# GLU groups between the memory attention's steps, and the next head's scores between transposes and values

## The chip, the cores and the metric

One core of one Trainium2 chip runs the whole program. The time is device microseconds (us) of one execution; lower is better. The core has five engines that run their own instruction queues and meet through semaphores: TensorE (PE in the profile), VectorE (DVE), ScalarE (ACT), GpSimd (POOL) and SyncE (SP, which here only issues DMAs). TensorE writes to PSUM (`ps`, eight banks of 512 floats per partition), and VectorE and ScalarE carry results on from there.

## What is computed

One decoder layer for a prompt of 1024 tokens and 32 sample tokens (8 x 4), so 1056 token columns. The part that matters here comes after the input projection: the gated linear unit behind the state-space branch, the cross-attention into 256 memory tokens, and the sparse attention of the prompt.

```python
# state-space branch: y is (tokens, 512), w_glu is (512, 1024)
a, g = jnp.split(y @ w_glu, 2, axis=-1)
o_s = a * jax.nn.sigmoid(g)
# memory attention: 4 heads of 128, 256 keys
s = jnp.einsum('bthd,bmhd->bhtm', q, mk) * (MEM_HEAD_DIM ** -0.5)
o_m = jnp.einsum('bhtm,bmhd->bthd', jax.nn.softmax(s, axis=-1), mv)
# prompt attention: 8 query heads, 2 KV heads of 128; ALiBi; a mask keeps the chosen keys
s = q @ k_sel * (HEAD_DIM ** -0.5) - slopes * dist          # -inf where not valid
o_a = jax.nn.softmax(s, axis=-1) @ v_sel
mix = concat(o_a * silu(gate_a), o_s * silu(gate_s), o_m * silu(gate_m))
```

All of it is float32 in this part of the kernel.

## The kernel before

The program is a row of blocks that each end in a barrier of all engines: setup, project, `mix_a` (`block_c`, from line 1267), `attend` (`block_d`, from line 1502), sample, out. The change touches `mix_a` and `attend`.

**`mix_a`.** SyncE issues all loads at once, in this order: `yT` (the state-space output), the first and the other columns of `w_glu`, the gates `gate_s` (into `mixT`, which lies in `y_room`), `kT`, `vT`, the memory keys and values `mem_kv`, the memory queries `qmT`, `gate_m`, and the attention gates `gate_a`. TensorE then goes through three pieces of work in a fixed order.

1. The GLU (L1370): twelve groups, for four chunks `c` of 128 output columns and the three token pieces of `HALVES` (512, 512 and 32 columns). A group is eight matmuls, four into one bank for `a` and four into the next for `g`. ScalarE takes the sigmoid of `g` (L1427), VectorE multiplies it by `a` (L1457) and into `mixT` (L1465). Two pairs of banks (0 and 1, 2 and 3) are used in turn.
2. The turning of keys and values by token (L1379, copied by ScalarE in L1431) and of the memory keys (L1384, copied by ScalarE in L1433 into `mkT`, a piece of `yT` that the GLU no longer needs).
3. The memory attention, over `s` with one tile of 128 queries each: logits of tile `s` (L1396, four matmuls of 256 columns), values of tile `s - 2` (L1407, eight of 128) and transposes of tile `s - 1` (L1417, eight of 128 x 128). Between them VectorE takes the maximum (L1471) and scales it (L1472), ScalarE takes four exponentials (L1440), VectorE inverts their sums (L1476) and multiplies (L1477), and the transposed weights are copied to `pmT`, one half by ScalarE (L1447) and one by VectorE (L1487). VectorE multiplies the result into `mixT` (L1483). It starts when all of the GLU is done (`glu_used` is waited for in full), since its weights `pm` and `pmT` lie in the room of `w_glu`.

**`attend`.** `UNITS` are 16 pairs of a query tile `t` (0 to 7) and a KV head `g`; unit `u` has `t + 1` key blocks. Step `s` computes the scores of unit `s`, one head `j` after the other (L1666, 128 queries against `(t + 1) * 128` keys); VectorE adds the distances, finds the maximum and writes `lg` (L1730), ScalarE writes the exponentials `pr` (L1697). Beside it unit `s - 1` is finished, cut into four parts by `steps`: "turn" a key block (L1641, four transposes into bank 4 or 5), have it copied to `prT` (L1683, blocks with even number by ScalarE, odd ones by VectorE), and "value" it (L1651, one matmul of 512 columns). A block's values follow one transpose later in TensorE's order. When a unit's values are done VectorE multiplies them into `mixT` (L1740), and GpSimd scales them by the inverse sums (L1631), which SyncE moves through DRAM. On that queue of SyncE also stand the loads of the queries two tiles on (`load_queries`, L1499) and the first loads of the sample block.

What orders ScalarE's queue in `attend`:

```python
for s in range(len(UNITS) + 1):
    for j in range(GQA):
        ...  # exponential of head j of unit s, waits for VectorE's s_read
        copy_turned(act, nc.scalar.copy, s - 1, todo[j], 0)
```

Of the kernel before, what the change touches and what calls it, by code (L numbers as in the profile page):

```python
# [16 lines left out]
P = 128  # L17
# [16 lines left out]
HALVES = [(0, 512), (512, 512), (SEQ, NS)]  # L34
# [12 lines left out]
SPAN = 8  # L47
# [1219 lines left out]
def block_c(nc, io, v, sem, sb_in):  # L1267
# [4 lines left out]
    with own:  # L1272
# [6 lines left out]
        sg = sb("sg", [P, 2, 512])  # L1279
        ag = sb("ag", [P, 512])  # L1280
# [20 lines left out]
        GLU = [(c, n) for c in range(4) for n in range(3)]  # L1301

# [57 lines left out]
        def _(pe):  # L1360
            pe.wait_ge(glu_loaded, 48)
            for i, (c, n) in enumerate(GLU):
                t0, w = HALVES[n]
                if (c, n) == (1, 0):
                    pe.wait_ge(glu_rest, 32)
                if i >= 2:
                    pe.wait_ge(glu_used, i - 1)
                for a in range(2):
                    for k in range(4):
                        last = nc.tensor.matmul(ps[:, 2 * (i % 2) + a, 0:w], w_glu[:, k, a * D_SSM + c * P:a * D_SSM + (c + 1) * P],  # L1370
                                                yT[:, k, t0:t0 + w], start=(k == 0), stop=(k == 3))
                last.then_inc(glu_mm, 1)
            pe.wait_ge(kv_loaded, 32)
# [14 lines left out]
            pe.wait_ge(glu_used, len(GLU))  # L1388
            pe.wait_ge(kv_copied, QT + 1)
            for s in range(QT + 2):  # L1390
                if s < QT:

                    if s >= 2:
                        pe.wait_ge(exp_done, 4 * (s - 1))
                    for h in range(N_MEM_HEADS):
                        last = nc.tensor.matmul(ps[:, 2 * (s % 2) + h // 2, (h % 2) * N_MEM:(h % 2 + 1) * N_MEM],  # L1396
                                                qmT[:, h, s * P:(s + 1) * P], mkT[:, h, :], start=True, stop=True)
                    last.then_inc(s_mm, 1)
                if s >= 2:
                    u = s - 2  # L1400
                    for k in range(2):
                        pe.wait_ge(p_copied[k], u + 1)
                    if u >= 2:
                        pe.wait_ge(o_used, u - 1)
                    for h in range(N_MEM_HEADS):
                        for k in range(2):
                            last = nc.tensor.matmul(ps[:, 6 + u % 2, h * P:(h + 1) * P], mem_kv[:, 1, k, h * P:(h + 1) * P],  # L1407
                                                    pmT[:, u % 2, k, h, :], start=(k == 0), stop=(k == 1))
                    last.then_inc(o_mm, 1)
                if 1 <= s <= QT:  # L1410
                    u = s - 1
                    pe.wait_ge(p_ready, u + 1)
                    for k in range(2):
                        if u >= 1:
                            pe.wait_ge(p_copied[k], u)
                        for h in range(N_MEM_HEADS):
                            last = nc.tensor.transpose(ps[:, 4 + k, h * P:(h + 1) * P], pm[:, u % 2, h, k * P:(k + 1) * P], ident[:])  # L1417
                        last.then_inc(p_turned, 1)

        @block.scalar  # L1420
        def _(act):
            for i, (c, n) in enumerate(GLU):
                w = HALVES[n][1]
# [3 lines left out]
                nc.scalar.activation(sg[:, i % 2, 0:w], ps[:, 2 * (i % 2) + 1, 0:w], ACT.Sigmoid).then_inc(glu_sig, 1)  # L1427
            for t in range(QT + 1):
                n = P if t < QT else NS
                act.wait_ge(kv_turned, t + 1)  # L1430
                nc.scalar.activation(kv_tok[0:n, t, :], ps[0:n, 4 + t % 2, :], ACT.Copy).then_inc(kv_copied, 1)  # L1431
            act.wait_ge(mk_turned, 1)
            nc.scalar.activation(yT[:, 0, 0:4 * N_MEM], ps[:, 6:8, :].rearrange("p a n -> p (a n)"), ACT.Copy).then_inc(mk_copied, 1)  # L1433
            for s in range(QT + 1):
                if s < QT:
# [3 lines left out]
                    for h in range(N_MEM_HEADS):  # L1439
                        nc.scalar.activation(pm[:, s % 2, h, :], ps[:, 2 * (s % 2) + h // 2, (h % 2) * N_MEM:(h % 2 + 1) * N_MEM],  # L1440
                                             ACT.Exp, bias=nb[:, s, h:h + 1], scale=SCALE, accum_out=rs[:, s, h:h + 1]).then_inc(exp_done, 1)
                if s >= 1:
                    u = s - 1
                    act.wait_ge(p_turned, 2 * u + 1)
                    if u >= 2:
                        act.wait_ge(o_mm, u - 1)
                    nc.scalar.activation(pmT[:, u % 2, 0, :, :].rearrange("p h n -> p (h n)"), ps[:, 4, :], ACT.Copy).then_inc(p_copied[0], 1)  # L1447

        @block.vector
        def _(dve):  # L1450
            link = v["dve_chain"].on(dve)
            TSC, TT = nc.vector.tensor_scalar, nc.vector.tensor_tensor
            dve.wait_ge(gate_s_loaded, 32)
            for i, (c, n) in enumerate(GLU):
                t0, w = HALVES[n]
                dve.wait_ge(glu_sig, i + 1)
                TT(ag[:, 0:w], ps[:, 2 * (i % 2), 0:w], sg[:, i % 2, 0:w], ALU.mult).then_inc(glu_used, 1)  # L1457
                dve.wait_ge(glu_used, i + 1)
                if n < 2:
                    o = mixT[:, 8 + c, 0:SEQ].rearrange("p (k j) -> p j k", j=SPAN)[:, t0 // BLKS:(t0 + w) // BLKS, :]  # L1460
                    x = ag[:, 0:w].rearrange("p (j k) -> p j k", k=BLKS)
                else:
                    o = mixT[:, 8 + c, SEQ:TOK].rearrange("p (b q) -> p q b", q=DEC_SEQ)
                    x = ag[:, 0:w].rearrange("p (q b) -> p q b", q=DEC_SEQ)
                link(TT(o, o, x, ALU.mult))  # L1465
            dve.wait_ge(gate_m_loaded, 32)
            for s in range(QT + 2):
                if s < QT:
                    dve.wait_ge(s_mm, s + 1)
                    src = ps[:, 2 * (s % 2):2 * (s % 2) + 2, :].rearrange("p a (h n) -> p (a h) n", h=2)  # L1470
                    link(nc.vector.tensor_reduce(nmx[:, s, :], src, AX_X, ALU.max, negate=True))  # L1471
                    TSC(nb[:, s, :], nmx[:, s, :], SCALE, None, ALU.mult).then_inc(nb_ready, 1)  # L1472
                if 1 <= s <= QT:
                    u = s - 1
                    dve.wait_ge(exp_done, 4 * (u + 1))
                    link(nc.vector.reciprocal(rinv[:, u, :], rs[:, u, :]))  # L1476
                    TT(pm[:, u % 2, :, :], pm[:, u % 2, :, :], rinv[:, u, :].unsqueeze(2).to_broadcast([P, 4, N_MEM]),  # L1477
                       ALU.mult).then_inc(p_ready, 1)
                if s >= 2:
                    u = s - 2  # L1480
# [3 lines left out]
                if 1 <= s <= QT:  # L1484
                    u = s - 1
                    dve.wait_ge(p_turned, 2 * u + 2)
# [1097 lines left out]
```

## Time and profile before

| | us |
|---|---|
| median of 3 runs (1938.87 to 1942.88) | 1939.59 |
| the profiled execution | 1938.08 |
| its span in the profile | 1936.3 |
| of it: GLU, 1154.07 to 1219.08 | 65.0 |
| turning of keys and memory keys, to 1227.03 | 8.0 |
| memory attention, to 1279.5 | 52.5 |
| prompt attention, 1280.5 to 1469.7 | 189.2 |

TensorE is busy for 93% of the span, VectorE for 52%, ScalarE for 42%, GpSimd for 15%. Engines are read as follows: a row of the time line gives the start, the duration, the engine, the line and the operation, and in brackets the idle time before it with what ended it. A matmul of float32 appears as two records. The records of TensorE overlap: the time between two starts is what one costs in a stream, and the duration of the last one holds its drain. PEclk is the share of TensorE's full clock of 2.4 GHz that was granted.

### The profile page before, as it was taken

The page shows a single profiled execution, that of the slowest core. Times are in us where ns is not written, and L with a number is a line of the kernel's source. Part 1 is how long each engine was busy: PE and PEld are TensorE (multiplying, and loading weights), DVE is VectorE, ACT ScalarE, POOL GpSimd, SP SyncE. Part 2 cuts the span into 40 slices and gives each one's busy share as a digit, 9 for nine tenths or more (in the row PEclk, how much of TensorE's full clock was granted, in tenths as well). Part 3 has the DMA queues.
Part 4 walks back from the last instruction along what each step waited for, and adds up shares of the span by engine and source line. Part 5 has one row for each costly group of instructions (what it writes and reads, how often), then busy time and mean ns, then how long its engine had stood idle before and what let it go on. Part 6 is the DMA issues. An engine that isn't in the chain of part 4 may idle for free. (4 is left out here: it accounts for less than half of the span.)

```text
span 1936.3 us, 30854 instructions
## 1 busy us (share of the span) xinstructions
PE 1802.8 (93%) x12571; PEld 1217.1 (63%) x12571; DVE 1013.2 (52%) x1945; ACT 817.3 (42%) x1386; POOL 294.0 (15%) x202
## 2 busy tenths in 40 slices
PE   6969999999999999999999979779889679999997
PEld 4555555556666666666666645664545368888886
DVE  5544126547978677687785602454435542222326
ACT  5454457764444334343433300444334744333431
POOL 3012220111121111111221100144103000000000
PEclk9989999999999999999999989989999799999999
DMA  9422221212223222222222146213215622222224
GB/s 331 141 88 66 72 66 34 67 45 78 74 70 94 80 75 78 80 84 78 78 74 75 51 149 253 67 26 85 66 34 158 205 67 67 89 67 67 68 89 180
DMA packets 193679, 179.82 MB, mean 93 GB/s; under 512 B 30658, under 2 KB 173154, under 8 KB 190786
## 3 DMA queue, kind: packets, MB, share of 16 engines
q1 hardware_dynamic: 174338, 140.29, 23.8%
q10 hardware_dynamic: 14640, 22.96, 3.2%
q0 software_dynamic: 4560, 14.58, 2.3%
q8 instruction: 101, 1.65, 0.4%
q14 instruction: 40, 0.33, 0.1%
HBM read 143.59 MB, written 34.20 MB: 92 GB/s over the span
## 5 line engine op out<-in xcount | busy, mean ns | idle before, releaser
L670 PE MATMUL ps<-h,w 128*128 128x352 f16 (+2 forms) x6096 | 943.9, 315 | 6.5 <-POOL w L950 6.1
L670 PEld LDWEIGHTS ps<-h,w 128*128 128x128 f16 (+1 forms) x6096 | 595.5, 99 | 337.9 <-issue 15.4
L950 POOL TENSOR_TENSOR w<-wb,w 128x2048 f16<-128x2048 f32 (+1 forms) x45 | 186.6, 4147 | 840.6 <-ACT w L802 840.6
L2372 PE MATMUL ps<-w_f,m 128*128 128x256 f16 x2688 | 297.0, 273 | 3.1 <-DVE y_room L2439 3.1
L2372 PEld LDWEIGHTS ps<-w_f,m 128*128 128x128 f16 x2688 | 263.1, 98 | 35.6 <-issue 4.6
L1152 DVE MAX8 m<-score 128x8 f32<-128x1024 f32 (+2 forms) x192 | 171.6, 894 | 5.7
L1153 DVE MATCH_REPLACE8 score<-m,score 128x1024 f32<-128x1024 f32 (+2 forms) x192 | 168.1, 876 | 0.0
L810 ACT ACTIVATE zst<-ps,unit 128x352 f32<-128x352 f32 (+1 forms) x88 | 50.0, 583 | 250.8 <-PE ps L670 226.7
L2454 DVE SCALAR_TENSOR_TENSOR y_room<-ps,unit_f,x_f 128x256 f32<-128x256 f32 (+1 forms) x64 | 30.6, 483 | 225.5 <-PE ps L2372 195.8
L1144 DVE SCALAR_TENSOR_TENSOR score<-room,wis,score 128x1024 f32<-128x1024 f32 (+5 forms) x90 | 92.7, 1030 | 78.6 <-ACT room L872 73.3
L798 ACT ACTIVATE wb<-wb,unit 128x2048 f32<-128x2048 f32 (+1 forms) x45 | 89.5, 1989 | 91.6 <-DVE unit L967 91.6
L784 ACT ACTIVATE absolute<-wb 128x512 bf16<-128x512 f32 (+1 forms) x180 | 112.5, 625 | 9.7 <-PEq L209 6.0
L872 ACT ACTIVATE room<-ps,qk_unit 128x1024 f32<-128x1024 f32 (+5 forms) x96 | 76.5, 845 | 54.9 <-PE ps L691 54.3
L1697 ACT ACTIVATE pr<-lg,nmx_d 128x128 f32<-128x128 f32 (+7 forms) x64 | 49.6, 776 | 107.7 <-DVE nmx_d L1730 107.3
L2515 ACT ACTIVATE qi_s<-y_room 128x256 bf16<-128x256 f32 (+3 forms) x72 | 29.6, 412 | 146.2 <-DVE y_room L2454 143.3
L1651 PE MATMUL ps<-prT,kv_tok 128*128 128x512 f32 x144 | 75.5, 612 | 15.5 <-ACT prT L1683 12.8
L802 ACT ACTIVATE w<-wb 128x2048 f16<-128x2048 f32 (+1 forms) x45 | 85.4, 1898 | 4.0
L1666 PE MATMUL ps<-kT,v_or_q 128*128 128x512 f32 (+3 forms) x192 | 75.4, 508 | 7.1 <-DMA v_or_q<-z_scratch 4.6
L1730 DVE CUSTOM_DVE_ANT_0 lg<-dist,ps 128x384 f32<-128x384 f32 (+5 forms) x48 | 42.6, 887 | 70.7 <-PE ps L1666 70.4
L1370 PE MATMUL ps<-yT,w_glu_sb 128*128 128x512 f32 (+1 forms) x192 | 65.2, 503 | 13.5 <-DMA w_glu_sb<-in_w_glu_dram 13.5
L961 DVE TENSOR_REDUCE unit<-ps 128x1 f32<-128x4 f32 x45 | 7.2, 161 | 117.6 <-PE ps L653 117.2
L1370 PEld LDWEIGHTS ps<-yT,w_glu_sb 128*128 128x128 f32 x192 | 32.7, 196 | 46.3 <-issue 32.4
(456 smaller groups left out, 1848.3 us busy)
## 6 DMA issues: line engine op xcount, KB each, us to landing
wb<-in_w_in_dram SPq DMA_DIRECT2D x44, 1024.0 KB, 5.2
z_scratch<-zst ACTq DMA_DIRECT2D x32, 528.0 KB, 2.7
score<-in_w_out_dram SPq DMA_DIRECT2D x7, 2048.0 KB, 11.5
y_room<-z_scratch SPq DMA_DIRECT2D x8, 1056.0 KB, 18.0
x_in<-in_x_prompt_dram SPq DMA_DIRECT2D x8, 1024.0 KB, 7.3
w_kv<-in_w_mem_kv_dram POOLq DMA_DIRECT2D x16, 512.0 KB, 5.3
x_f<-in_x_prompt_dram SPq DMA_DIRECT2D x8, 1024.0 KB, 5.3
out_y_p_dram<-y_room SPq DMA_DIRECT2D x8, 1024.0 KB, 3.9
```

What stands on the lines that cost most here:

```text
L670: last = nc.tensor.matmul(ps[0:m, n, 0:w], w16[:, b, pw_, k, 0:m], h16[:, ph, k, t0:t0 + w], start=(k == 0 and i == 0), stop=(k == KT - 1 ...
L784: nc.scalar.activation(absolute[:, :, 0:w], wb[:, b, 4 * k:4 * k + 4, 0:w], ACT.Abs, accum_out=size[:, b, k:k + 1]).then_inc(w_summed, 1)
L798: nc.scalar.activation(src, src, ACT.Copy, scale=unit[:, c % 4, 1:2]).then_inc(act_link, 1)
L802: nc.scalar.activation(high, src, ACT.Copy).then_inc(w_high, 1)
L872: nc.scalar.activation(rel[:, a, 0:(t + 1) * P], src, ACT.Relu, scale=qk_unit[:, 1 + i:2 + i]).then_inc(act_read, 1)
L950: nc.gpsimd.tensor_tensor(w16[:, b, 1, :, 0:w], wb[:, b, :, 0:w], w16[:, b, 0, :, 0:w], ALU.subtract).then_inc(w_split, 1)
L1144: STT(out=sc, in0=r, scalar=wi, in1=sc, op0=ALU.mult, op1=ALU.add).then_inc(acc_done, 1)
L1152: link(nc.vector.max(out=m8[:], in_=sc))
L1153: link(nc.vector.match_replace(out=sc, in_to_replace=m8[:], in_values=sc, imm_value=REPLACED))
L1370: last = nc.tensor.matmul(ps[:, 2 * (i % 2) + a, 0:w], w_glu[:, k, a * D_SSM + c * P:a * D_SSM + (c + 1) * P], yT[:, k, t0:t0 + w], start= ...
L1651: nc.tensor.matmul(ps[:, 6 + u % 2, :], v_, prT[:, gk % 2, :, :].rearrange("p j n -> p (j n)"), start=(k == 0), stop=(k == t)).then_inc(o_ ...
L2372: last = nc.tensor.matmul(ps[:, bank(b, t), 0:SLAB], m16[:, mp, k, t * P:(t + 1) * P], weights(s, b, wp, k), start=(k == 0 and j == 0), st ...
```

## The change

In `mix_a` the token pieces of the GLU become 384, 384 and 288 columns. Three of its twelve groups stay ahead of the memory attention (two before the turning of keys and values, one after), and one of the other nine stands in each of the nine steps of the memory attention, between the transposes of tile `s - 1` and its values, which now belong to the same step. All groups but the second use banks 2 and 3, and the logits have banks 0 and 1 alone. `mkT`, `pm` and `pmT` move out of `yT` and `w_glu`: `mkT` to the unused end of `y_room`, `pm` to `k_room`, `pmT` (now one buffer in place of two) to the room of the memory keys. Sigmoids and exponentials alternate on ScalarE. In `attend` a block's values come after the next head's scores, VectorE's product with the gate moves to the start of the next step but one, and there is one step more.

```diff
-HALVES = [(0, 512), (512, 512), (SEQ, NS)]
+THIRDS = [(0, 384), (384, 384), (768, 256 + NS)]
...
-        mkT = yT[:, 0, 0:4 * N_MEM].rearrange("p (h n) -> p h n", h=4)
-
-        pm = w_glu[:, 0:2, :].rearrange("p b (h n) -> p b h n", h=4)
-        pmT = w_glu[:, 2:4, :].rearrange("p b (k h n) -> p b k h n", k=2, h=4)
+        mkT_flat = v["y_room"][:, KT * TOK:KT * TOK + 4 * N_MEM]
+        mkT = mkT_flat.rearrange("p (h n) -> p h n", h=4)
+
+        pm = v["k_room"][:].rearrange("p (b h n) -> p b h n", b=2, h=4)
+        pmT = mem_kv[:, 0, :, :].rearrange("p k (h n) -> p k h n", h=4)
...
+        GLU_FIRST = 3
+        def glu_bank(i):
+            return 0 if i == 1 else 2
...  # TensorE: glu(i) as before, but
-                    pe.wait_ge(glu_used, i - 1)
+                    pe.wait_ge(glu_used, i)
...
+            pe.wait_ge(glu_loaded, 48)
+            glu(0)
+            glu(1)
             pe.wait_ge(kv_loaded, 32)
...
+            glu(2)
             pe.wait_ge(mem_loaded, 64)
...
-            pe.wait_ge(glu_used, len(GLU))
             pe.wait_ge(kv_copied, QT + 1)
-            for s in range(QT + 2):
+            for s in range(QT + 1):
                 if s < QT:
-                    ...  # logits(s), values(s - 2), transposes(s - 1)
+                    logits(s)
+                if s:
+                    turn(s - 1)
+                glu(GLU_FIRST + s)
+                if s:
+                    values(s - 1)
...  # ScalarE, in a step: copy of tile s - 1 to pmT, four exponentials of tile s, then
+                gate(GLU_FIRST + s)
...  # VectorE, in a step: maximum of tile s, copy to pmT, inverse sums and product of tile s, then
+                multiply(GLU_FIRST + s)
+                if s >= 1:
+                    ...  # product of tile s - 1 into mixT
...  # attend
-        def steps(u):
-            ...
+        STEPS = len(UNITS) + 2
+        def blocks(u, j):
+            if not 0 <= u < len(UNITS):
+                return []
             kb = UNITS[u][0] + 1
+            return [(u, k) for k in range(kb * j // GQA, kb * (j + 1) // GQA)]
+        def turned_at(s, j):
+            return blocks(s - 1, j)
+        def valued_at(s, j):
+            return turned_at(s, j - 1) if j else turned_at(s - 1, GQA - 1)
...  # TensorE, after the scores of head j
-                    if s and j == 0:
+                    for u, k in valued_at(s, j):
+                        value(u, k)
+                    if j == 0 and 1 <= s <= len(UNITS):
                         pe.wait_ge(exp_done, GQA * s)
-                    for kind, k in todo[j]:
-                        (turn if kind == "turn" else value)(s - 1, k)
+                    for u, k in turned_at(s, j):
+                        turn(u, k)
...  # VectorE, after the copies of part j
+                    if j == 0 and s >= 2:
+                        gate(s - 2)
-                if s:
-                    ...  # the same product, for unit s - 1, at the end of step s
```

## Rows read from the trace of the kernel before

**Rows 1.** Busy time by stage: us, PE, PEld, DVE, ACT, POOL, PEclk, DMA share, GB/s.
```profile
1154.07:1219.08 65.01, 65.01 (x193) 32.60 (x193) 14.49 (x22) 5.38 (x11) 0.00 (x0) 0.96 0.60 235
1219.08:1227.03 7.95, 5.98 (x46) 4.57 (x46) 1.46 (x3) 6.18 (x12) 1.80 (x1) 1.00 0.02 4
1227.03:1279.50 52.47, 40.69 (x256) 36.56 (x256) 31.70 (x47) 21.39 (x73) 3.76 (x2) 0.93 0.20 61
1280.50:1331.44 50.94, 44.19 (x161) 25.58 (x162) 26.05 (x89) 24.25 (x72) 34.52 (x57) 0.93 0.30 70
1331.44:1469.70 138.26, 123.46 (x465) 67.26 (x463) 58.09 (x110) 48.87 (x93) 24.46 (x13) 0.99 0.23 51
```

**Rows 2.** Waits of PE, 1154 to 1280: who for whom, us, times, longest.
```profile
PE ps L1417 <- DVE w_glu_sb L1477: 10.1, 7, 3.6
```

**Rows 3.** Time line of PE in one step of the memory attention.
```profile
1241.75 1.10 PE L1417 MATMUL ps<-ident,w_glu_sb 128*128 128x128 f32 x8 [1.08 <-DVE w_glu_sb L1477]
1242.68 1.89 PE L1396 MATMUL ps<-yT,qmT 128*128 128x256 f32 x8
1244.41 1.95 PE L1407 MATMUL ps<-w_glu_sb,mem_kv 128*128 128x128 f32 x16
```

**Rows 4.** Time line of ACT: the sigmoids of the first three GLU groups.
```profile
1164.12 0.60 ACT L1427 ACTIVATE sg<-ps 128x512 f32<-128x512 f32 x1 [18.52 <-PE ps L1370]
1170.99 0.60 ACT L1427 ACTIVATE sg<-ps 128x512 f32<-128x512 f32 x1 [6.27 <-PE ps L1370]
1172.69 0.20 ACT L1427 ACTIVATE sg<-ps 128x32 f32<-128x32 f32 x1 [1.11 <-PE ps L1370]
```

**Rows 5.** Busy time by stretch, as rows 1: PEclk after two waits of PE.
```profile
1154.00:1158.00 4.00, 3.93 (x5) 1.85 (x6) 0.00 (x0) 0.00 (x0) 0.00 (x0) 0.50 1.08 382
1234.40:1238.50 4.10, 4.10 (x15) 3.54 (x16) 0.69 (x1) 0.88 (x3) 0.00 (x0) 0.58 0.94 307
```

**Rows 6.** Time line of SP's queue: when two of the loads are issued.
```profile
1153.14 0.46 SPq L1322 DMA_DIRECT2D v_or_q<-z_scratch  x1
1157.60 5.06 SPq L1327 DMA_DIRECT2D qmT<-z_scratch  x2
```

**Rows 7.** DMA issues of the same loads: KB each, us from issue to landing.
```profile
v_or_q<-z_scratch SPq DMA_DIRECT2D x1, 1056.0 KB, 16.1
qmT<-z_scratch SPq DMA_DIRECT2D x2, 1056.0 KB, 16.9
```

**Rows 8.** Time line of ACT: the table load ahead of the first exponential.
```profile
1227.00 1.28 ACT L1440 ACT_TABLE_LOAD   x1
1230.92 0.47 ACT L1440 ACTIVATE w_glu_sb<-ps,nb_c 128x256 f32<-128x256 f32 x1 [2.65 <-DVE nb_c L1472]
```

**Rows 9.** Groups by line, memory attention: count, busy us, mean ns, idle before.
```profile
L1471 DVE TENSOR_REDUCE nmx_c<-ps 128x4 f32<-128x1024 f32 x8 | 9.8, 1225 | 16.1 <-PE ps L1396 16.1
L1440 ACT ACTIVATE w_glu_sb<-ps,nb_c 128x256 f32<-128x256 f32 x32 | 14.7, 476 | 22.5 <-DVE nb_c L1472 22.5
```

**Rows 10.** Waits of PE in the prompt attention, 1331 to 1470.
```profile
PE ps L1651 <- ACT prT L1683: 12.2, 10, 2.2
```

**Rows 11.** Time line of PE, DVE and ACT at one of these waits.
```profile
1440.59 1.04 PE L1641 MATMUL ps<-ident,pr 128*128 128x128 f32 x8
...
1440.79 1.22 DVE L1730 CUSTOM_DVE_ANT_0 lg<-dist,ps 128x1024 f32<-128x1024 f32 x1 [1.03 <-PE ps L1666]
...
1442.06 1.15 ACT L1697 ACTIVATE pr<-lg,nmx_d 128x1024 f32<-128x1024 f32 x1 [3.68 <-DVE nmx_d L1730]
...
1443.82 0.70 PE L1651 MATMUL ps<-prT,kv_tok 128*128 128x512 f32 x1 [2.19 <-ACT prT L1683]
```

**Rows 12.** Groups by line and shape, prompt attention: the 640-key head.
```profile
L1730 DVE CUSTOM_DVE_ANT_0 lg<-dist,ps 128x640 f32<-128x640 f32 x8 | 6.6, 822 | 8.6 <-PE ps L1666 8.5
L1697 ACT ACTIVATE pr<-lg,nmx_d 128x640 f32<-128x640 f32 x8 | 6.6, 830 | 11.6 <-DVE nmx_d L1730 11.5
```

**Rows 13.** Time line of PE: the first scores of tile 3.
```profile
1314.73 1.12 PE L1666 MATMUL ps<-kT,v_or_q 128*128 128x512 f32 x2 [1.24 <-DMA v_or_q<-z_scratch]
```

More of the change, by code:

```diff
@@ L1360, in _, with glu @@
         def _(pe):
-            pe.wait_ge(glu_loaded, 48)
-            for i, (c, n) in enumerate(GLU):
-                t0, w = HALVES[n]
+            def glu(i):
+                c, n = GLU[i]
+                t0, w = THIRDS[n]
                 if (c, n) == (1, 0):
@@ L1387, in _, with gate @@
             pe.wait_ge(mk_copied, 1)
-            pe.wait_ge(glu_used, len(GLU))
             pe.wait_ge(kv_copied, QT + 1)
-            for s in range(QT + 2):
+            for s in range(QT + 1):
                 if s < QT:
[L1393 to L1418, printed above, removed]
+                    logits(s)
+                if s:
+                    turn(s - 1)
+                glu(GLU_FIRST + s)
+                if s:
+                    values(s - 1)
         @block.scalar
         def _(act):
-            for i, (c, n) in enumerate(GLU):
-                w = HALVES[n][1]
+            def gate(i):
+                w = THIRDS[GLU[i][1]][1]
                 act.wait_ge(glu_mm, i + 1)
@@ L1452, in _, with multiply @@
             TSC, TT = nc.vector.tensor_scalar, nc.vector.tensor_tensor
-            dve.wait_ge(gate_s_loaded, 32)
[L1454 to L1465, printed above, removed]
+            def multiply(i):
+                c, n = GLU[i]
+                t0, w = THIRDS[n]
+                dve.wait_ge(glu_sig, i + 1)
+                TT(ag[:, 0:w], ps[:, glu_bank(i), 0:w], sg[:, i % 2, 0:w], ALU.mult).then_inc(glu_used, 1)
+                dve.wait_ge(glu_used, i + 1)
+                w_p = min(w, SEQ - t0)
+                o = mixT[:, 8 + c, 0:SEQ].rearrange("p (k j) -> p j k", j=SPAN)[:, t0 // BLKS:(t0 + w_p) // BLKS, :]
+                x = ag[:, 0:w_p].rearrange("p (j k) -> p j k", k=BLKS)
+                last = TT(o, o, x, ALU.mult)
+                if w_p < w:
+                    o = mixT[:, 8 + c, SEQ:TOK].rearrange("p (b q) -> p q b", q=DEC_SEQ)
+                    x = ag[:, w_p:w].rearrange("p (q b) -> p q b", q=DEC_SEQ)
+                    last = TT(o, o, x, ALU.mult)
+                link(last)
@@ L1466, in _ @@
+            dve.wait_ge(gate_s_loaded, 32)
+            for i in range(GLU_FIRST):
+                multiply(i)
             dve.wait_ge(gate_m_loaded, 32)
-            for s in range(QT + 2):
+            for s in range(QT + 1):
                 if s < QT:
                     dve.wait_ge(s_mm, s + 1)
-                    src = ps[:, 2 * (s % 2):2 * (s % 2) + 2, :].rearrange("p a (h n) -> p (a h) n", h=2)
+                    src = ps[:, 0:2, :].rearrange("p a (h n) -> p (a h) n", h=2)
                     link(nc.vector.tensor_reduce(nmx[:, s, :], src, AX_X, ALU.max, negate=True))
@@ L1652, in value @@
                                  start=(k == 0), stop=(k == t)).then_inc(o_mm, 1)
-            for s in range(len(UNITS) + 1):
-                todo = steps(s - 1) if s else [[]] * 4
+            for s in range(STEPS):
                 for j in range(GQA):
@@ L1668, in _, with copy_turned @@
                         last.then_inc(s_mm, 1)
-                    if s and j == 0:
+                    for u, k in valued_at(s, j):
+                        value(u, k)
+                    if j == 0 and 1 <= s <= len(UNITS):
                         pe.wait_ge(exp_done, GQA * s)
-                    for kind, k in todo[j]:
-                        (turn if kind == "turn" else value)(s - 1, k)
-        def copy_turned(eng, copy, u, todo, parity):
-            for kind, k in todo:
+                    for u, k in turned_at(s, j):
+                        turn(u, k)
+        def copy_turned(eng, copy, todo, parity):
+            for u, k in todo:
                 gk = first_key_block[u] + k
-                if kind == "turn" and gk % 2 == parity:
+                if gk % 2 == parity:
                     eng.wait_ge(p_turned, gk + 1)
@@ L1687, in _ @@
             for s in range(len(UNITS) + 1):
-                todo = steps(s - 1) if s else [[]] * 4
                 for j in range(GQA):
@@ L1713, in invert, with gate @@
                 nc.vector.reciprocal(rinv[:, GQA * u:GQA * (u + 1)], rs[:, GQA * u:GQA * (u + 1)]).then_inc(rinv_ready, 1)
-            for s in range(len(UNITS) + 1):
-                todo = steps(s - 1) if s else [[]] * 4
+            def gate(u):
+                t, g = UNITS[u]
+                dve.wait_ge(o_mm, first_key_block[u + 1])
+                o = mixT[:, GQA * g:GQA * (g + 1), t * P:(t + 1) * P]
+                nc.vector.tensor_tensor(o, o, ps[:, 6 + u % 2, :].rearrange("p (j n) -> p j n", j=GQA), ALU.mult).then_inc(o_used, 1)
+            for s in range(STEPS):
                 for j in range(GQA):
```

90 lines of the change are left out of this document (52 added, 38 removed).

## The prediction

> **What bounds the kernel now.** I read the stages by busy time first [rows 1]. Both stages that the change touches are TensorE's, and in both it stops for short times. In the GLU it never stops: 65.01 us busy in 65.01. In the memory attention it is busy for 40.69 of 52.47 us, and the clock is 0.93. In the prompt attention after 1331.44 it is busy for 123.46 of 138.26. Then the waits, to see on whom: in the memory attention on VectorE's product with the inverse sums (10.1 us) [rows 2], in the prompt attention mostly on ScalarE's copy of transposed weights (12.2 us) [rows 10]. So the softmax of a tile, or the copy of a block, has too little of TensorE's work beside it. The GLU is such work, 65 us with no stop, and stands ahead of the attention that could use it.
>
> **The GLU's own cost.** A 512-column group takes 1170.99 - 1164.12 = 6.87 us from sigmoid to sigmoid, a 32-column group 1172.69 - 1170.99 = 1.70 [rows 4]. Eight and four of them are 61.8 us; the 3.2 us that are left of 65.01 are the start at half clock (0.50) after the wait for the first loads [rows 1, 5], and stay. The new pieces by columns: 384 cost 5.15, 288 cost 3.87; eight and four are 56.7. Gain **5.1**.
>
> **The memory attention's steps.** From start to start the transposes take 0.93 us and the logits 1.73 [rows 3]; the values have as many columns as the logits, so 1.73 too (their 1.95 holds the drain that follows them now). A step's own work is 4.39 us, eight tiles 35.1, against 52.47 us now [rows 1]: **17.4** go if the GLU group in each step covers all waits. Does it? A step is 4.39 + 5.15 = 9.54 us, or 8.26 with a 288-column group. The softmax chain of a tile: logits 1.73, maximum 1.23, four exponentials of 0.476, product 1.23 (an estimate: as many elements as the maximum) [rows 9], some five hand-overs of 0.20 each as between TensorE and VectorE [rows 11]: 7.1 us. Its result is wanted by the next step's transposes, at 8.26 + 1.73 = 10.0 at the earliest. Covered by 2.9 us.
>
> What is added in a step: on ScalarE a sigmoid and two table switches, since sigmoid and exponential each load a table now; one load takes 1.28 us. The load at 1227.00 ran ahead of the wait of its exponential, which began at 1230.92 [rows 8], so I expect the loads in ScalarE's idle time; even with one on the chain it is 8.4 against 10.0. ScalarE's sum is 1.9 + 0.45 + 2.56 + 0.6 for the copy (an estimate from what follows the exponential in rows 11) = 5.5 of 8.26 us. That row speaks for hidden switches. The Trainium skill, "ScalarE: Activation LUTs", section "Table sets: the hidden batching unit", speaks against them: calls are to be batched by set, and a switch is budgeted at about 2.7 us, by which ScalarE's sum would be 8.3, just over the short step. The trace has 1.28 for the load itself; the rule as a result of its own is the second rival.
>
> The new waits: TensorE waits for VectorE's product of the last GLU group (`glu_used`), since all later groups share banks 2 and 3. Behind it are the values and the next logits. The group ends 7.81 us into a step; sigmoid and product follow by about 9.5 (they stand behind the softmax product of 7.1 to 8.4), and the next group begins at 8.26 + 2.66 = 10.9 or later. Covered by 1.4 us or more. Behind VectorE's wait for the sigmoid stand the gate product of tile s - 1 and the next maximum; the latter has until 9.99. Covered, thinly.
>
> The loads: two GLU groups in front take 3.2 + 10.3 us from 1154.07, to 1167.6. `vT` lands at 1153.14 + 16.1 = 1169.2 [rows 6, 7]: a new wait of about **1.7** us that the long GLU hid. `qmT` lands by about 1177.3 (its second half is issued 2.5 us into the row) [rows 6, 7]; the turning (7.95) [rows 1] and the third group put the first logits at 1167.6 + 1.7 + 7.95 + 3.87 = 1181.1 and the turning of the memory keys, which waits for it, some 2 us earlier. Hidden by 1.8 us. After a wait of 3.6 us the clock fell to 0.58 [rows 2, 5], so the 1.7 us may cost up to 2 more. Values at 1.95 instead of 1.73 would take 1.8. The same tail as now remains at the end. Sum 5.1 + 17.4 - 1.7 = 20.8; with part of these bounds I take **20** (16 to 21).
>
> SyncE's and GpSimd's queues only have the attention gates, the queries and the scaling of `kT`, which start earlier and end before the stage does. The moved rooms cost no instruction.
>
> **The prompt attention.** From the end of the scores to the values that wait for ScalarE's copy it takes 1443.82 - 1440.59 = 3.23 us at 1024 keys (VectorE 1.22, exponential 1.15, copy and hand-overs the rest); eight transposes cover 1.04 of it, and the wait is 2.19 [rows 11]. After the change the previous blocks' values, this part's transposes and the next head's scores lie between. By 1.73 us for 1024 columns [rows 3] a block's values (512 columns) are 0.865, scores 0.216 for 128 keys, and a block's transposes about 0.44 [rows 11]. At 1024 keys two blocks a part: 1.73 + 0.88 + 1.73 = 4.34 against 3.23. Covered. At 640 keys one block: 0.865 + 0.44 + 1.08 = 2.39, against 3.23 less the difference of both engines (0.40 + 0.32) [rows 11, 12] = 2.51: short by 0.1. So about nothing remains but small waits at tiles 4 and 5, some 1 us in all. In the last step no scores are left: a part's values wait for a copy behind one transposed block, about 0.5 us for each of four parts, 2 us.
>
> The sum from 1331.44: scores 8 heads x (5 + 6 + 7 + 8) x 0.216 = 44.9; 56 blocks' transposes x 0.44 = 24.6; values 57 x 0.865 = 49.3 (one more, since they lag); waits 3: 121.8, against 138.26: **16.5**. From the other side: busy 123.46 [rows 1] plus 3 and 0.9 is 127.4, a gain of 10.9; but busy time holds the drain before each wait, which goes with it. I take **15.5**, near the first.
>
> Before 1331.44 I expect nothing. The scores of tile 3 wait for their queries [rows 13], and what TensorE saves before it waits there: SyncE's queue reaches these loads behind GpSimd's set-up work, which does not change. After it the cover at 512 keys (0.865 + 0.44 + 0.86 = 2.17) is about what the chain needs (2.27 by the same differences), so waits like today's stay. Bounds -2 to +1.5 us; value 0. VectorE's gate product moves in front of the second head of a step; there it delays that head's maximum by up to 0.3 us in the middle tiles. The block ends with the same product and GpSimd's scaling. The later stages start earlier and are unchanged.
>
> **Sum.** 20 + 15.5 = 35.5. The profiled execution took 1938.08 (span 1936.3), 1.5 below the median 1939.59; so 1902.6 for that one and **1904** for the median.
>
> **Rivals.**
> - Forecast, 1904, own range 1898 to 1910: chance 0.62.
> - The prompt attention keeps half its waits: VectorE's order (maximum, copies, gate product) or the scores' own semaphore makes ScalarE's copy late again. For it: the margin at 640 keys is below zero and 0.35 at 896; against: 1.1 us at 1024, where most waits are. Half of 15.5: 1912. Chance 0.17.
> - The table switches lie on the path: 16 more loads x 1.28 = 20.5 us [rows 8]: 1924.5. Against it, the load that ran ahead of its wait. Chance 0.07. The Trainium skill's rule (above) names this outcome; by its 2.7 us it would be 43 us, and no gain at all.
> - The loads fall behind and each us late is a us of waiting, or the clock falls in the turning: up to 6 us, 1910. Chance 0.10.
> - Slower than before: the one pair of banks. If each of nine groups had to wait for VectorE's product of the last, TensorE would stop in every step, and after 3.6 us it ran near half clock for 4 us (0.58, some 1.7 us lost) [rows 5]. Nine waits of 3 us with that loss are 42 us: 1946. It decides from 35.5 / 9 = 3.9 us per step, loss included, and needs VectorE 1.4 us of margin plus 2.2 late. Chance 0.04.
>
> That the change doesn't do what it says is hardly possible; the order of the instructions is written out.
>
> The range for 8 in 10 reaches from the forecast's low end over the second and fourth rival: 1898 to 1914. This kernel's measurement tells about 0.2% (4 us) from no change; faster 0.95, same 0.01, slower 0.04.
>
> **What would show it.** The stretch from the first GLU matmul to the last values should take about 105.5 us (125.4 now), with TensorE busy for all but some 3 us and no wait on VectorE's product; some 17 table loads on ScalarE, none ahead of a wait of TensorE; one wait for `vT` of about 1.7 us. In the prompt attention the waits on ScalarE's copy should fall from 12.2 us to about 3, most of them in the last step, and tile 3 should begin 34 us into the block as now. I am wrong if TensorE waits for `glu_used` or for a sigmoid in the steps, if the waits on the copy move to VectorE's, or if the clock in the steps is below 1.00.

## The result, and the profile after

| | before | after |
|---|---|---|
| median us (runs) | 1939.23 (1938.10 to 1942.88, 4) | 1904.77 (1902.38 to 1906.13, 4) |
| profiled execution, span | 1938.08, 1936.3 | 1904.64, 1903.0 |
| first GLU matmul to last values of the memory attention | 125.4 | 106.1 |
| from there to the first matmul of the stage after the prompt attention | 193.2 | 177.2 |
| all that follows | 463.6 | 465.4 |

After / before is 0.9823, with a 95% interval of 0.9810 to 0.9836: 34.5 us gained. By the stages of the two traces it is 19.3 and 16.0, less 1.8 lost in stages that the change doesn't touch. Of the 19.3 some 3 us are the clock in the trace of before, as shown below under "Luck".

Busy time by stage in the kernel after (start:end, us, then busy us and count of PE, PEld, DVE, ACT, POOL, then PEclk, DMA share, GB/s): first two GLU groups and the turning of keys and values; third group and steps; the prompt attention up to the first scores of tile 4; the rest of it. Rows 1 has the stages of before.

```profile
1154.29:1176.35 22.06, 18.44 (x68) 11.80 (x69) 2.82 (x4) 5.48 (x10) 0.00 (x0) 0.86 1.04 402
1176.35:1260.36 84.01, 82.89 (x426) 64.35 (x424) 45.35 (x71) 47.12 (x101) 5.55 (x2) 1.00 0.32 116
1261.49:1312.47 50.98, 44.55 (x158) 24.21 (x159) 25.78 (x88) 25.40 (x72) 34.29 (x57) 0.93 0.32 69
1312.47:1434.88 122.41, 120.92 (x468) 67.66 (x466) 59.54 (x111) 49.08 (x94) 24.66 (x13) 1.00 0.25 58
```

The second line is the merged stage: TensorE is busy for 82.89 of 84.01 us at full clock, where the memory attention alone had 40.69 of 52.47 at 0.93 [rows 1]. The last is 122.41 us, against 138.26 [rows 1].

The waits of TensorE in the kernel after (engine, line, releaser: us in total, times, longest), first for 1154 to 1262, then for 1262 to 1450:

```profile
PE ps L1421 <- DMA v_or_q<-z_scratch: 3.3, 1, 3.3
PE ps L1386 <- ACT y_room L1459: 1.1, 1, 1.1
...
PE ps L1691 <- ACT prT L1724: 3.9, 8, 0.9
PE ps L1705 <- DMA v_or_q<-z_scratch: 1.7, 2, 1.1
PE ps L1691 <- DVE prT L1724: 0.7, 3, 0.3
```

The 10.1 us for VectorE's product [rows 2] are gone, and no line for `glu_used` or a sigmoid has come. The 12.2 us for ScalarE's copy, which rows 10 count from tile 4 on, are 1.4 there (after 1312.47). The other 2.5 of the 3.9 us lie ahead of tile 4, where before had 0.6; there the wait for queries fell in turn, from 4.6 to 1.7. What is new is 3.3 us for `vT`.

One step of the memory attention on TensorE, DVE and ACT (start, us, engine, line, operation, with idle time before it and its releaser in brackets):

```profile
1207.19 1.89 PE L1386 MATMUL ps<-y_room,qmT 128*128 128x256 f32 x8
1208.92 1.04 PE L1397 MATMUL ps<-ident,k_room 128*128 128x128 f32 x8
1209.80 5.33 PE L1377 MATMUL ps<-yT,w_glu_sb 128*128 128x384 f32 x16
1214.96 1.95 PE L1408 MATMUL ps<-mem_kv 128*128 128x128 f32 x16
1216.74 1.89 PE L1386 MATMUL ps<-y_room,qmT 128*128 128x256 f32 x8
...
1209.12 1.23 DVE L1505 TENSOR_REDUCE nmx_c<-ps 128x4 f32<-128x1024 f32 x1 [0.28 <-PE ps L1386]
1210.38 0.17 DVE L1506 TENSOR_SCALAR nb_c<-nmx_c 128x4 f32<-128x4 f32 x1
1213.64 1.22 DVE L1516 TENSOR_TENSOR k_room<-k_room,rinv_c 128x1024 f32<-128x1024 f32 x1
...
1209.56 0.60 ACT L1466 ACTIVATE mem_kv<-ps 128x512 f32<-128x512 f32 x1 [2.71 <-PE ps L1397]
1210.17 1.28 ACT L1472 ACT_TABLE_LOAD   x1
1211.47 0.47 ACT L1472 ACTIVATE k_room<-ps,nb_c 128x256 f32<-128x256 f32 x1
1213.42 1.28 ACT L1449 ACT_TABLE_LOAD   x1
1215.16 0.49 ACT L1449 ACTIVATE sg<-ps 128x384 f32<-128x384 f32 x1 [0.46 <-PE ps L1377]
```

TensorE's five lines follow each other with no bracket: 1216.74 - 1207.19 = 9.55 us for the step. The chain goes beside them: the product (L1516) ends at 1214.86, and the next transposes want it at 1216.74 + 1.73 = 18.47. The exponential's load starts behind ScalarE's copy (L1466) and ends 0.9 us after the scaled maximum (1210.55), so this load is partly on the chain; 3.6 us of margin absorb it. The thinnest place is VectorE's: it waits only 0.28 us for these logits, as forecast ("thinly").

One 1024-key head of the prompt attention after the change, the same columns; rows 11 has it before:

```profile
1404.57 1.22 DVE L1775 CUSTOM_DVE_ANT_0 lg<-dist,ps 128x1024 f32<-128x1024 f32 x1 [1.03 <-PE ps L1705]
1405.83 1.15 ACT L1737 ACTIVATE pr<-lg,nmx_d 128x1024 f32<-128x1024 f32 x1 [2.59 <-DVE nmx_d L1775]
1406.08 1.04 PE L1681 MATMUL ps<-ident,pr 128*128 128x128 f32 x8
1406.95 1.88 PE L1705 MATMUL ps<-kT,v_or_q 128*128 128x512 f32 x4
1406.98 0.56 ACT L1724 COPY prT<-ps 128x512 f32<-128x512 f32 x1
1408.67 1.88 PE L1691 MATMUL ps<-prT,kv_tok 128*128 128x512 f32 x4
```

The copy (L1724) still stands behind the exponential on ScalarE and ends at 1407.54. But the values that need it start at 1408.67, behind the next head's scores, and don't wait.

### The profile page after: what moved, and what is told of

It is laid out like the page before. It is cut to its first block and busy times, and to the rows that moved or that the text cites. A ratio compares the mean times of both kernels' runs of the same rounds, so it can differ in the third digit from the quotient of the medians.

```text
span 1903.0 us, 30882 instructions
## 1 busy us (share of the span) xinstructions
PE 1793.9 (94%) x12571; PEld 1221.9 (64%) x12571; DVE 1014.7 (53%) x1949; ACT 837.6 (44%) x1402; POOL 293.8 (15%) x202
## 5 line engine op out<-in xcount | busy, mean ns | idle before, releaser
L1377 PE MATMUL ps<-yT,w_glu_sb 128*128 128x384 f32 (+1 forms) x192 | 60.1, 468 | 13.4 <-DMA w_glu_sb<-in_w_glu_dram 13.4
L990 DVE SCALAR_TENSOR_TENSOR room<-ps,room 128x400 f16<-128x400 f32 (+1 forms) x16 | 8.9, 558 | 93.8 <-ACT room L818 53.2
```

## The experiments

All medians are of timed runs beside the kernel before; the ratio is against it, with its 95% interval. The rows come from three sets of runs, and the result from a fourth; the median of before was 1939.1 (mix_alone to no_switch), 1938.5 (two_more_switches, copies_first, kv_sooner, three_more), 1938.4 (the other three) and 1939.2 us (the result). Differences between sets are uncertain by that much beside their spread.

| kernel | us | ratio |
|---|---|---|
| mix_alone | 1922.13 | 0.9917 (0.9900 to 0.9934) |
| attend_alone | 1921.19 | 0.9905 (0.9889 to 0.9922) |
| glu_ahead | 1921.29 | 0.9912 (0.9895 to 0.9928) |
| no_switch | 1903.48 | 0.9810 (0.9794 to 0.9827) |
| two_more_switches | 1913.86 | 0.9873 (0.9855 to 0.9891) |
| copies_first | 1926.68 | 0.9935 (0.9916 to 0.9954) |
| mix_and_copies | 1904.47 | 0.9832 (0.9816 to 0.9848) |
| after_copies_first | 1904.02 | 0.9823 (0.9807 to 0.9840) |
| kv_sooner | 1902.25 | 0.9810 (0.9794 to 0.9826) |
| queries_sooner | 1901.64 | 0.9812 (0.9796 to 0.9829) |
| three_more | 1897.31 | 0.9783 (0.9767 to 0.9800) |

**Are the two parts independent?** mix_alone has the diff's part up to the memory attention, attend_alone its part in the prompt attention.

> The kernel before with only the change of the first block: GLU groups in the memory attention's steps, the prompt attention as before. Theory: the two stages gain apart from each other; the stretch from the first GLU matmul to the last values falls from 125.4 to 106.1 us and nothing later changes, so 1939.2 - 19.3 = 1920 (1918 to 1922). Rival: the stages depend on one another (the prompt attention starts on queries that are loaded at a fixed time, so part of the gain is waited for there): 1925 or more.

> The kernel before with only the change of the prompt attention. Theory: the wait for ScalarE's copies goes, 12.2 us to about 4, and the block takes 173.4 in place of 189.3 us: 1939.2 - 16 = 1923 (1921 to 1925), with nothing gained before the scores of tile 4. Rival: part of the 16 us came from the first block's change (its earlier end moves transfers away): 1928 or more.

They gained 17.0 and 17.9 us. The first, 1922.13, is just outside the range expected for it. Together they make 34.9, against 34.5 for the whole change: within the spread of some 3 us, neither part needs or spoils the other.

**Is it the GLU beside the attention, or the new order of a step?** glu_ahead keeps the step's new order, its rooms and its pieces, but puts all twelve groups in front:

```diff
-            return 0 if i == 1 else 2
+            return 2 * (i % 2)
...
-            glu(0)
-            glu(1)
+            for i in range(len(GLU)):
+                glu(i)
...
-                glu(GLU_FIRST + s)
```

> The changed kernel, but all twelve GLU groups ahead of the turning of keys and values, with two pairs of banks in turn; the steps have the new order (logits, transposes of the tile before, its values) and no GLU in them. Theory: the groups' cover is the gain; without it a step is bound by the softmax chain (logits 1.73, maximum 1.23, table-free exponentials 1.9, hand-overs, then the next logits wait for the exponentials): about 5.5 us a step as before (5.7), so the 14 us of the steps are lost again and the thinner pieces' 5 us stay: 1918 to 1922. Rival: the new order of the steps and the shorter lag did it, and the place of the groups matters little: 1905 to 1908.

It gained 17.8, as attend_alone does: with the GLU in front, nothing of the 17 us of mix_alone shows in the medians. In the trace the GLU takes 59.05 us instead of 65.01 and the memory attention 53.86 (before 52.47 [rows 1]). From the first GLU matmul to the last values it is 120.7 us, 4.7 less than in the trace of before, but only 1.4 less than in that of attend_alone (122.1), which has the code of before there. One step of it, TensorE and the VectorE instructions that matter:

```profile
1250.12 1.04 PE L1397 MATMUL ps<-ident,k_room 128*128 128x128 f32 x8
1252.45 2.02 PE L1408 MATMUL ps<-mem_kv 128*128 128x128 f32 x16 [1.29 <-issue]
1254.31 1.89 PE L1386 MATMUL ps<-y_room,qmT 128*128 128x256 f32 x8
...
1250.32 1.23 DVE L1502 TENSOR_REDUCE nmx_c<-ps 128x4 f32<-128x1024 f32 x1 [0.45 <-PE ps L1386]
1251.66 0.69 DVE L1509 COPY mem_kv<-ps 128x512 f32<-128x512 f32 x1
```

The values (L1408) wait 1.29 us. The profile names no releaser here, but VectorE's copy of the second half of the transposed weights (L1509) ends at 1252.35, 0.1 us ahead of them, and it stood behind the maximum; for the waits of 1.33 and 1.34 us of two earlier tiles it names this copy. The new order alone shows no gain; its waits are hidden only where a group lies in them.

**Do the table loads cost anything?** no_switch:

```diff
-                ... ACT.Sigmoid).then_inc(glu_sig, 1)
+                ... ACT.Exp).then_inc(glu_sig, 1)
```

> The changed kernel with an exponential in place of the sigmoid in the GLU's gate, which leaves the sigmoid out and with it all 16 added table loads (20.5 us of ScalarE). Theory: ScalarE has 3 to 4 us to spare in each step and the loads are hidden: 1904.8, within 1. Rival: the loads lengthen the chain to TensorE by 0.8 us or more a step: 1898 or less.

1903.48 against 1904.77: no difference that these runs can tell (their spread is 4 us). The traces are closer: from the first logits to the last values no_switch takes 77.98 us and after 77.97. 16 loads of 1.28 us, 20.5 us in all, are hidden. How near to the edge? two_more_switches puts two loads more on every tile's chain:

```diff
                         nc.scalar.activation(pm[:, s % 2, h, :], ... ACT.Exp, ...).then_inc(exp_done, 1)
+                        if h == 1:
+                            nc.scalar.activation(spare_col[:], ident[:, 0:1], ACT.Sigmoid)
```

> The changed kernel with one more sigmoid of one column between the second and the third exponential of each of the eight tiles; its result is not used. It adds two table loads and about 0.3 us, 2.9 us a step, in the middle of the softmax chain, where they can't run ahead. Theory: VectorE's round of a step (maximum, scaling, the exponentials waited for, inverse, product, GLU product twice, gate product) takes about 8 us of 9.5 or 8.3, so 0.3 us are free in a short step and 1.5 in a long one; 2.9 more cost some 1.5 us in each long and 2.6 in each short step, 12 to 15 us: 1917 to 1920. Rival 1: the cover is wide (the product is wanted only 2.3 us later than it is there), at most 3 us: 1905 to 1908. Rival 2: ScalarE's loads are on TensorE's path already, so all of it is paid: 8 x 2.9 = 23 us, 1928.

It lost 9.1 us against after, where 12 to 15 were expected and the nearest rival had at most 3. TensorE's waits are before the logits, since one pair of banks holds them and the last exponential must have read it:

```profile
PE ps L1387 <- ACT k_room L1473: 5.2, 4, 1.7
PE ps L1398 <- DVE k_room L1519: 1.9, 1, 1.9
```

A loop through VectorE and ScalarE now sets the step. DVE and ACT of one step, with the maximum of the step before it, show it:

```profile
1206.38 1.22 DVE L1508 TENSOR_REDUCE nmx_c<-ps 128x4 f32<-128x1024 f32 x1
1216.33 1.22 DVE L1508 TENSOR_REDUCE nmx_c<-ps 128x4 f32<-128x1024 f32 x1
1222.66 0.18 DVE L1518 RECIPROCAL rinv_c<-rs_c 128x4 f32<-128x4 f32 x1 [4.32 <-ACT k_room L1473]
1224.46 0.56 DVE L1488 TENSOR_TENSOR ag<-ps,sg 128x384 f32<-128x384 f32 x1 [0.37 <-ACT sg L1450]
1226.57 1.22 DVE L1508 TENSOR_REDUCE nmx_c<-ps 128x4 f32<-128x1024 f32 x1
...
1215.82 1.28 ACT L1473 ACT_TABLE_LOAD   x1
1217.78 0.47 ACT L1473 ACTIVATE k_room<-ps,nb_c 128x256 f32<-128x256 f32 x1 [0.68 <-DVE nb_c L1509]
1218.82 1.28 ACT L1476 ACT_TABLE_LOAD   x1
1220.11 0.20 ACT L1476 ACTIVATE spare_col<-ident 128x1 f32<-128x1 f32 x1
1220.32 1.28 ACT L1473 ACT_TABLE_LOAD   x1
```

From maximum to maximum it is 10.24 us in this step, which has a 384-column group, and 9.95 in the one before it, which has 288 columns; VectorE waits for ScalarE alone. Less the 2.9 us of the added chain (two loads and the small sigmoid) that is about 7.3 and 7.1, so the 9.55 us step had 2.2 free and the 8.27 us step 1.2. The loss is 0.7 us in a long and 1.7 in a short step, where 1.5 and 2.6 were expected. My expectation counted only VectorE's idle time ahead of the maximum (0.28 above). It missed that a later maximum takes the exponential's own load off the chain: the load now ends at 1217.10, before the wait (0.68 idle), where it cost 0.9 us in after. 0.28 + 0.9 is the 1.2 of the short step.

**What made the copies late in the prompt attention?** The prediction laid the wait to the length of the chain, to be covered by TensorE's work. The rival: the copy is ready to go long before, and stands behind an exponential on ScalarE that waits for VectorE. copies_first changes the kernel before in that one point and leaves TensorE's order as it was:

```diff
+                    copy_turned(act, nc.scalar.copy, s - 1, todo[j], 0)
                     if s < len(UNITS):
                         n = (UNITS[s][0] + 1) * P
...
-                    copy_turned(act, nc.scalar.copy, s - 1, todo[j], 0)
```

> The kernel before with one edit in the prompt attention: ScalarE's copies of a part stand ahead of the exponential of its head, not behind it. Theory: the waits of TensorE came from the place of the copy behind an exponential; with it gone a value waits 0.8 us less the 0.44 of one transposed block, so the 12.2 us fall to about 5 and the block gains about 7: 1930 to 1933. Rival: what lacks is work of TensorE between transposes and values, whatever ScalarE's order; the exponential, now later, holds up the next tile instead: 1938 to 1941.

It gained 11.8 us; I expected about 7. TensorE's waits from 1331 to 1456, and one head's time line:

```profile
PE ps L1651 <- DVE prT L1683: 2.6, 5, 1.1
PE ps L1651 <- ACT prT L1683: 1.2, 5, 0.2
...
1428.14 1.04 PE L1641 MATMUL ps<-ident,pr 128*128 128x128 f32 x8
1428.77 0.58 ACT L1683 COPY prT<-ps 128x512 f32<-128x512 f32 x1 [2.85 <-PE ps L1641]
1429.41 1.13 PE L1651 MATMUL ps<-prT,kv_tok 128*128 128x512 f32 x2 [0.24 <-ACT prT L1683]
```

The copy runs 0.63 us after the first transposes begin, in time in which ScalarE was idle anyway (2.85), and the values wait 0.24 us instead of 2.19 [rows 11]. Of 12.2 us [rows 10] 1.2 are left. I had expected part of the wait to stay for the chain, and hardly any did. mix_and_copies puts this beside the other half of the change, with TensorE's order in the prompt attention left as before:

```diff
 (mix_alone, and in the prompt attention of before:)
+                    copy_turned(act, nc.scalar.copy, s - 1, todo[j], 0)
                     if s < len(UNITS):
```

> The kernel before with the first block's change and, in the prompt attention, only ScalarE's copies put ahead of the exponentials; TensorE's order there is that of before. Theory: the copy's place behind the exponential made nearly all of the waits, and either cure removes them; the block takes 177.6 us from its first score to the next block's first matmul against 176.1 with the new order of TensorE: 1904.8 + 1.5 = 1906 (1904 to 1909). Rival: TensorE's order gives more once the first block ends 19 us sooner, since other transfers then fall into the block: 1912 or more.

1904.47 against 1904.77 for the change: the same total. The prompt attention itself isn't the same. From its first scores to the next stage's first matmul the traces have:

| kernel | us |
|---|---|
| before | 192.1 |
| mix_alone (order of before) | 191.2 |
| copies_first | 177.6 |
| mix_and_copies | 179.2 |
| attend_alone (new order) | 176.0 |
| after (new order) | 176.1 |

The moved line gives 14.5 us of the 16.2 that the new order gives, and beside the first block's change 12.0 of 15.1. The medians of the two alone differ as well (1926.68 and 1921.19). In the two traces the totals come out level because the later stages of mix_and_copies took 461.3 us, against 465.4 in after. What the new order covers besides is the waits for VectorE's copies: 2.6 us from tile 4 on, in before as in copies_first (above) and in mix_and_copies, and none there in after:

```profile
PE ps L1687 <- DVE prT L1719: 2.6, 5, 1.1
```

after_copies_first has both cures (the copy's line moved as above, in the kernel after):

> The changed kernel with ScalarE's copies ahead of the exponentials. Theory: of the 3.9 us of waits for copies that are left, 2.5 us lie at tiles 1 and 2, where the queries bound the start of the next tile, so little of them is won: 1903 to 1905, and the waits for queries grow from 1.7 to 3 us or more. Rival: all of them go: 1901 or less.

1904.02: no more than the new order alone. Its waits on the copy fell from 3.9 to 1.4 us, and the one for the queries rose from 1.7 to 4.8:

```profile
PE ps L1705 <- DMA v_or_q<-z_scratch: 4.8, 2, 2.6
PE ps L1691 <- ACT prT L1724: 1.4, 6, 0.2
```

Nearly all of those 2.5 us (2.3) were at tiles 1 and 2, where the loads set the pace, so they came back at once.

**The waits for loads.** kv_sooner issues `kT` and `vT` ahead of the state-space gates; queries_sooner issues each tile's queries one unit earlier:

```diff
+            sp.dma_start(kT[:], pair(OFF_K)).then_inc(kv_loaded, 16)
+            sp.dma_start(vT[:], pair(OFF_V)).then_inc(kv_loaded, 16)
             for s in range(2):
                 sp.dma_start(mixT[:, 8 + 2 * s:10 + 2 * s, :], pair(OFF_GS + SLAB * s)).then_inc(gate_s_loaded, 16)
...
-                if g == 0 and 1 <= t < QT - 1:
-                    sp.wait_ge(s_mm, N_HEADS * t)
-                    load_queries(sp, q_t, z_dram, t + 1, q_loaded)
+                if g == 1 and t + 2 < QT:
+                    sp.wait_ge(s_mm, N_HEADS * (t + 1))
+                    load_queries(sp, q_t, z_dram, t + 2, q_loaded)
```

> The changed kernel with the loads of keys and values issued ahead of the GLU's gates. Theory: the wait of 3.3 us for the values and the half clock after it go (about 1 us more); the third group then ends before the memory queries are there, about 1.5 us of waiting comes back: 2.5 to 3 us less, 1902. Rival: the GLU's product, whose gates now land 5 us later, holds up the third group: no change, 1904.8 or more.

> The changed kernel with the queries of the tile after next issued one unit sooner on SyncE's queue. Theory: the 1.7 us of waits for queries go and nothing else: 1903 (1902 to 1904.5). Together with the run before, less than the 5 us that both edits gave on top of the sooner keys: each needs the other, since the copies and the queries bound the first tiles in turn. Rival: the two edits add up, and this one gives 2.5 us or more: 1902 or less.

Against after they gained 2.5 and 3.1 us; by the ratios it is 2.5 and 2.1. The first is within the spread of the runs (1900.1 to 1905.2, against 1902.4 to 1906.1); the runs of the second (1901.2 to 1901.9) all lie below those of after. Its median is below the range expected for it and in that of its rival, but the trace shows the 1.7 us of the theory and no more. The traces agree that both gain. With kv_sooner the 3.3 us for `vT` are gone and a wait of 1.1 us for `qmT` is new:

```profile
PE ps L1427 <- DMA qmT<-z_scratch: 1.1, 1, 1.1
```

With queries_sooner no wait for queries is left, and the prompt attention takes 174.4 us instead of 176.1, first scores to the next stage's first matmul. three_more has both, and the copies first:

> The changed kernel with three edits of order: keys and values loaded ahead of the GLU's gates, the queries of the tile after next issued one unit sooner on SyncE's queue, and ScalarE's copies ahead of the exponentials. Theory: besides the 3 us of the loads, the 4.6 us of waits for copies and the 1.7 us for queries at the first tiles shrink by about 4 together: 1897 to 1900. Rival: at the first tiles the chain from scores to exponential bounds, and a later exponential costs what the sooner copy gives: 1902, as with the loads alone.

1897.31 (1894.1 to 1899.0): 7.5 us less than the change, and the best of all. The single gains (2.5, 3.1 and 0.8) make 6.4. The prompt attention takes 170.8 us, 3.6 less than with queries_sooner alone, though kv_sooner (176.3) and after_copies_first (176.3) left it as it was: with the queries there in time, the copies' place pays, which it could not in after_copies_first. So the edits don't simply add up, and the rival of queries_sooner falls.

## Why the prediction was right, point by point

| term | predicted | measured in the trace of after |
|---|---|---|
| first two GLU groups | 13.5 | 11.99 |
| wait for `vT` | 1.7 | 3.33 |
| turning, third group, memory keys | 11.8 | 12.78 |
| steps | 35.1 + 42.5 = 77.6 | 77.97 |
| first GLU matmul to last values | 105.5 (104.6 by the terms above) | 106.1 |
| tile 3 into its block | 34 | 33.9 |
| prompt attention from tile 4 | 121.8 | 122.41 |
| later stages | unchanged | 1.8 longer |
| profiled execution | 1902.6 | 1904.64 |

- **Steps.** The step at 1.73 us for 1024 columns, with the drain left out, was right to 0.4 us in 78; the bound of 1.8 for slower values was not used. TensorE is busy for all of 77.97 us.
- **The wait for `vT`** is the mis-sized term: 3.33 for 1.7. The load landed as computed from rows 6 and 7 (1169.6 against 1169.2). The two groups in front took 1.5 us less, since the start at half clock cost less than the 3.2 us taken from before: the granted clock of the first 4 us is 0.61 instead of 0.50 [rows 5]. In the four us behind those it is 1.00 instead of 0.76. With the landing fixed the two errors cancel. What doesn't cancel is the clock after the wait, for which the prediction had up to 2 us: 0.75 and then 0.56 in the next 5 us, and the stretch to the first logits 1.0 us longer than forecast. Stretches of the kernel after, columns as above:

```profile
1169.60:1172.00 2.40, 2.14 (x13) 1.91 (x14) 0.00 (x0) 1.09 (x2) 0.00 (x0) 0.75 1.06 398
1172.00:1174.50 2.50, 2.50 (x13) 1.92 (x11) 0.00 (x0) 1.79 (x3) 0.00 (x0) 0.56 1.02 409
```

- **Table loads.** Right that they are hidden, and how: 8 loads for sigmoids and 8 for exponentials in the memory attention, as forecast about 17 with the one of the prompt attention, and no wait of TensorE behind one. Right for the exponential's load only by margin, since it ends 0.9 us late; the forecast had it wholly in idle time or wholly on the chain. The rival that put 20.5 us on the path falls by no_switch. Loads aren't free everywhere: two more per tile, put into the middle of the chain, cost 9.1 us over eight tiles. The Trainium skill, "ScalarE: Activation LUTs", section "Table sets: the hidden batching unit", asks to batch calls by set and puts a table load at about 2.7 us. The traces differ: a load takes 1.28 us, the next activation starts right behind it (1218.82 and 1220.11 in two_more_switches), and breaking the batches up cost nothing here.
- **Prompt attention.** The size was right (16.0 for the stage, and 15.85 from tile 4 on, against 15.5), and the last step keeps 1.4 us of waits where 2 were forecast. The reason was half right. The prediction counted what TensorE must put beside a chain of 3.23 us. The runs show that the chain need not have been waited for: the copy's place behind the exponential made the wait for ScalarE, and one line moved gives back most of what the new order gives (12.0 of 15.1, or 14.5 of 16.2 us). The rest fits the 2.6 us of waits for VectorE's copies, to which the prediction gave no term of their own; no run takes these out alone. The rival "attention keeps half its waits" falls with it.
- **Tiles 1 and 2** have 2.5 us of waits on ScalarE's copies, up from 0.6, which the prediction didn't name; they cost nothing while the queries bind (after_copies_first). The stretch up to tile 4 is as long as before (50.98 against 50.94), as forecast.
- **The pair of banks** never stopped TensorE: the product of a group ends 2.4 to 3.1 us before the next group starts, and 1.3 to 1.4 us before the groups of the second and the last step; at least 1.4 was forecast.
- **Later stages** were forecast unchanged and are 1.8 us longer in the trace of after. That is within what the same stages vary by (below), so it is no effect of the change that these runs can tell.
- **Luck.** The 125.4 us from the first GLU matmul to the last values, from which the prediction starts, hold a slow clock. The same code took 122.1 us in the trace of attend_alone and 122.5 in copies_first. Of the 3.3 us between before and attend_alone 2.0 lie in the memory attention, where the granted clock was 0.97 in attend_alone instead of 0.93 [rows 1], and 1.3 in the GLU:

```profile
1229.26:1279.69 50.43, 38.67 (x256) 34.80 (x256) 31.71 (x47) 21.35 (x73) 3.75 (x2) 0.97 0.21 64
```

  The changed stage took 105.0 to 106.2 us in the five traces that have it as it is in after. So 16 to 20 us are gained there, depending on the trace of before, and mix_alone's 17.0 is at the lower end of that. The prediction's 20 is read from a slow trace; that the sum came within 1 us of the measured gain is in part luck.

## What to carry to other kernels

Work of the bound engine that has no waits of its own belongs between the steps of work that has them; count the chain against it step by step, with the loop through the other engines (here 7.1 us of 8.3 and 7.3 of 9.6), which sets the least step. Before covering a wait, look at the releaser's queue: if the instruction that ends the wait stands behind another that itself waits, moving it is one line and may be most of the gain. And when compute moves ahead of a load, the load becomes the next wait: order its issue anew in the same change.

## What the runs showed of the hardware that was not expected

- The stages behind the prompt attention, the same in all kernels, took 461.3 to 467.4 us over the profiled executions, with no relation to the edits that I can see (463.6 before, 465.4 after, 467.4 with kv_sooner, 461.3 with mix_and_copies). One part shows in the clock. Before and after have the same wait of 2.7 us there, and in the 3.4 us after it the granted clock was 0.69 in before and 0.50 (1.2 GHz, the lower level, throughout) in after (before first):

```profile
1472.67:1476.07 3.40, 3.33 (x49) 1.47 (x49) 0.36 (x3) 1.17 (x2) 1.88 (x2) 0.69 0.19 46
1437.56:1440.96 3.40, 3.40 (x45) 2.34 (x49) 0.36 (x3) 1.17 (x2) 1.87 (x2) 0.50 0.17 45
```

  So the same wait costs a different time from one execution to the next. Another part is one wait of TensorE for a load of memory keys (`k_room`), of 3.8 us in before, 4.5 in after, 5.8 with kv_sooner and, with mix_and_copies, 1.1 and another 1.5 for a second load. What makes up the rest of the 6 us is open.
- The price of a table load isn't fixed: the exponential's load cost the chain 0.9 us in after, where ScalarE's copy came late ahead of it, and nothing in two_more_switches, where the step was longer (1215.82 above).
